# Attention probabilities transposed by VectorE in 32x32 squares instead of by TensorE and a ScalarE copy

## What is computed

```python
x = x + 0.5 * swiglu(rmsnorm(x, norm_ffn1[l]), w1_gate[l], w1_up[l], w1_down[l])
h = rmsnorm(x, norm_mix[l])
proj = h @ w_in[l]
q, k, v, u = jnp.split(proj, [ATTN_WIDTH, 2 * ATTN_WIDTH, 3 * ATTN_WIDTH], axis=-1)
...
    s_own = jnp.einsum('bhqd,bhpd->bhqp', qc, k_own).astype(jnp.float32) * scale
    s_own = jnp.where(k_pos[None, :] <= q_pos[:, None], s_own, NEG_INF)
    p = jax.nn.softmax(jnp.concatenate([s_sel, s_own], axis=-1), axis=-1)
...
            + jnp.einsum('bhqp,bhpd->bhqd', p_own, v_own))
...
pooled = multiscale_pool(u, pool_w[l], pool_scale[l])
x = x + jnp.concatenate([attn, pooled], axis=-1) @ w_out[l]
x = x + 0.5 * swiglu(rmsnorm(x, norm_ffn2[l]), w2_gate[l], w2_up[l], w2_down[l])
```

## The kernel before

| piece | engine | work | line |
|---|---|---|---|
| 36 | PE | scores q·k, two matmuls | L508 |
| 40 | DVE | scale and mask, row maxima | L1208, L1213 |
| 41 | ACT | exponential with row sums | L829 |
| 41 | DVE | reciprocal, rows scaled: `probs` | L1220, L1225 |
| 39 | PE | three 128x128 transposes of `probs` into PSUM | L520 |
| 43 | ACT | copy to SBUF: `probsT` | L837 |
| 43 | PE | values: v·`probsT`, two matmuls | L530, L532 |
| 47 | ACT | rounding into `h` | L842 |
| 48 | DVE | rest into `h`, signals `attn_ready` | L1231 |

## Time and profile before

### The profile page before, as it was taken

One profiled execution on the slowest core, in us unless ns is written; L12 is line 12 of the kernel. 1 busy time (PEld: TensorE's weight loads), 2 busy tenths in 40 slices (PEclk: granted clock), 3 DMA queues, 4 the chain that ended last, 5 costly groups with the idle time before them and its releaser, 6 DMA issues.

```text
span 1743.6 us, 20419 instructions
## 1 busy us (share of the span) xinstructions
PE 1733.9 (99%) x7878; PEld 1442.8 (83%) x7878; DVE 1118.7 (64%) x1378; ACT 782.5 (45%) x892; POOL 20.4 (1%) x24
## 2 busy tenths in 40 slices
PE   9999999999999999999999999999999999999998
PEld 7888888888888888888888888888888888888886
DVE  5666666666665566577676866666666666654554
ACT  6444444444444444454544555444444444443443
POOL 0000000000000000000040000000000000000000
PEclk9999999999999999999999999999999999999999
DMA  8555555555555555666544555555555555565552
GB/s 292 194 193 192 193 193 193 192 193 193 194 196 193 193 194 194 213 195 193 169 161 154 193 192 193 194 192 193 193 192 192 192 192 192 200 210 193 193 193 97
DMA packets 174257, 334.51 MB, mean 192 GB/s; under 512 B 5672, under 2 KB 17408, under 8 KB 174080
## 3 DMA queue, kind: packets, MB, share of 16 engines
q1 hardware_dynamic: 172608, 332.51, 56.2%
q10 hardware_dynamic: 1600, 1.32, 0.2%
HBM read 331.71 MB, written 2.10 MB: 191 GB/s over the span
## 4 chain that ended last, share of the span: by engine, by line
PE 99%; DMA 0%; DVE 0%; ACT 0%; SPq 0%; issue 0%; ACTq 0%
PE banks L389 30%; PE banks L391 30%; PE banks L390 30%; PE banks L375 5%; PE banks L378 3%; PE banks L545 0%; DMA raw<-in_w_gate 0%; PE banks L508 0%; PE banks L530 0%; PE banks L520 0%; PE banks L427 0%; PE banks L532 0%; PE banks L442 0%; DVE w_lo L881 0%; ACT w_hi L651 0%
## 5 line engine op out<-in xcount | busy, mean ns | idle before, releaser
L881 DVE TENSOR_TENSOR w_lo<-raw,w_hi 128x1024 fp32r<-128x1024 f32 x623 | 762.7, 1226 | 590.3 <-ACT w_hi L651 589.0
L651 ACT ACTIVATE w_hi<-raw 128x1024 fp32r<-128x1024 f32 x623 | 659.6, 1060 | 924.7 <-PE banks L391 848.2
L389 PE MATMUL banks<-w_hi,act 128*128 128x512 f32 x1468 | 572.7, 390 | 0.3 <-DVE act L895 0.3
L391 PE MATMUL banks<-w_lo,act 128*128 128x512 f32 x1468 | 571.4, 389 | 0.0
L390 PE MATMUL banks<-w_hi,act 128*128 128x512 f32 x1468 | 571.3, 389 | 0.0
L389 PE MATMUL banks<-w_hi,h 128*128 128x512 f32 x832 | 324.3, 390 | 0.0
L390 PE MATMUL banks<-w_hi,h 128*128 128x512 f32 x832 | 323.8, 389 | 0.0
L391 PE MATMUL banks<-w_lo,h 128*128 128x512 f32 x832 | 323.7, 389 | 0.0
L389 PEld LDWEIGHTS banks<-w_hi,act 128*128 128x128 f32 x1468 | 275.6, 188 | 57.5 <-DVE act L895 0.5
L391 PEld LDWEIGHTS banks<-w_lo,act 128*128 128x128 f32 x1468 | 275.5, 188 | 57.3
L390 PEld LDWEIGHTS banks<-w_hi,act 128*128 128x128 f32 x1468 | 275.6, 188 | 56.7
(11 more groups left out here) (125 smaller groups left out, 372.2 us busy)
## 6 DMA issues: line engine op xcount, KB each, us to landing
raw<-in_w_up SPq DMA_DIRECT2D x88, 1024.0 KB, 5.0
raw<-in_w_down SPq DMA_DIRECT2D x88, 1024.0 KB, 5.0
raw<-in_w_gate SPq DMA_DIRECT2D x84, 1024.0 KB, 5.0
raw<-in_w_in SPq DMA_DIRECT2D x32, 1024.0 KB, 5.4
raw<-in_w_out SPq DMA_DIRECT2D x16, 1024.0 KB, 5.0
raw<-in_w_gate SPq DMA_DIRECT2D x7, 512.0 KB, 8.7
xr<-in_x SPq DMA_DIRECT2D x8, 256.0 KB, 8.1
out<-out_rows SPq DMA_DIRECT2D x8, 256.0 KB, 2.5
```

What stands on the lines that cost most here:

```text
L389: pe.matmul(dst, operand[:, k, hi], w_hi[:, s, w], start=k == first, stop=False)
L391: mm = pe.matmul(dst, operand[:, k, hi], w_lo[:, s, w], start=False, stop=k == last)
L651: act_e.activation(w_hi[:, s, :], raw[:, (p // 2) % RAW_SLOTS, off:off + PIECE], ACT.Copy).then_inc(hi_ready, 1)
L881: dve.tensor_tensor(w_lo[:, s, :], raw[:, (p // 2) % RAW_SLOTS, off:off + PIECE], w_hi[:, s, :].bitcast(F32), ALU.subtract).then_inc(lo_re ...
```

## The change

The three transposes on TensorE (L520) and ScalarE's copy (L837) go away, with the semaphore between them. In their place VectorE writes `probsT` straight from `probs` in SBUF, 16 instructions for each head: each takes 32 partitions and 32 columns of each of the three blocks (32 x 96 values). They are given out in two parts of eight, at VectorE's pieces 42+3·hd and 43+3·hd. VectorE no longer waits for TensorE's transposes before it overwrites `probs`, and the values of head 0 take over the wait for `quad_read`, which the first transpose had.

```diff
-SCORES_AT, TURN_AT, VALUES_AT = 36, 39, 43
+SCORES_AT, TURN_AT, VALUES_AT = 36, 42, 43
...
-            def head_turn(hd):
-
-                pe.wait_ge(probs_ready, hd + 1)
-                if hd == 0:
-                    pe.wait_ge(quad_read, 4)
-                else:
-                    pe.wait_ge(probsT_ready, hd)
-                for j in range(3):
-                    mm = pe.transpose(banks[:, 2, j * P:(j + 1) * P],
-                                      probs[:, hd % 2, j * P:(j + 1) * P], ident[:, :])
-                mm.then_inc(probs_turned, 1)
-
             def head_values(hd):
                 pe.wait_ge(probsT_ready, hd + 1)
                 pe.wait_ge(v_ready, 2 if hd < 4 else 4)
+                if hd == 0:
+                    pe.wait_ge(quad_read, 4)
                 if hd >= 1:
                     pe.wait_ge(attn_ready, hd)
...
-                    hd = (p - TURN_AT - 4) // HEAD_STEP
-                    if (p - TURN_AT - 4) % HEAD_STEP == 0 and 0 <= hd < HEADS:
-                        act_e.wait_ge(probs_turned, hd + 1)
-                        if hd >= 2:
-                            act_e.wait_ge(values_ready, hd - 1)
-                        act_e.activation(probsT[:, hd % 2, :], banks[:, 2, 0:3 * P],
-                                         ACT.Copy).then_inc(probsT_ready, 1)
...
+            def turn_probs(hd, part):
+
+                dve.wait_ge(probs_ready, hd + 1)
+                if hd >= 2:
+                    dve.wait_ge(values_ready, hd - 1)
+                for m in range(8 * part, 8 * part + 8):
+                    i, j = m // SB, m % SB
+                    rows, cols = slice(j * SQ, (j + 1) * SQ), slice(i * SQ, (i + 1) * SQ)
+                    ins = dve.transpose(
+                        probsT[cols, hd % 2, :].rearrange("p (b q) -> p b q", b=3)[:, :, rows],
+                        probs[rows, hd % 2, :].rearrange("p (b q) -> p b q", b=3)[:, :, cols])
+                if part == 1:
+                    ins.then_inc(probsT_ready, 1)
...
-                        if hd >= 2:
-                            dve.wait_ge(probs_turned, hd - 1)
                         dve.wait_ge(scores_ready, hd + 1)
...
+                    for part in range(2):
+                        hd = (p - TURN_AT - part) // HEAD_STEP
+                        if (p - TURN_AT - part) % HEAD_STEP == 0 and 0 <= hd < HEADS:
+                            turn_probs(hd, part)
```

More of the change, by code:

```diff
@@ L242, in layer_kernel @@
         probs_ready = sem("probs_ready")
-        probs_turned = sem("probs_turned")
         probsT_ready = sem("probsT_ready")
@@ L609, in middle @@
                         head_scores((p - SCORES_AT) // HEAD_STEP)
-                    if (p - TURN_AT) % HEAD_STEP == 0 and 0 <= (p - TURN_AT) // HEAD_STEP < HEADS:
-                        head_turn((p - TURN_AT) // HEAD_STEP)
                     if (p - VALUES_AT) % HEAD_STEP == 0 and 0 <= (p - VALUES_AT) // HEAD_STEP < HEADS:
```

## The result

The changed kernel takes 1754.53 us (median of 4 runs, 1753.56 to 1755.27) against 1745.71 us before: 1.0049 times the time, 95% interval 1.0037 to 1.0061, so 8.8 us slower. The forecast was 1756.2 us, in a range of 1751 to 1762.

What follows compares the result with a forecast made beforehand. TensorE, busy 99% of the span, was taken to bound the kernel until VectorE's new work, 37.9 us, exceeded its 27.4 us reserve; the 10.5 us excess on the median gave 1756.2 us, range 1751 to 1762, TensorE's saved 2.6 us vanishing in waits.

Steps and rivals of the forecast that it cites:

- VectorE's reserve of 27.4 us: VectorE's idle time before its splits, from piece 42's split to head 7's write; new work would use it up.
- the fall of the clock: Rival: TensorE's clock drops to half speed behind its new waits, at most 16 us on top, 1772 us; 5%.
- the signs that were to show me wrong: Transpose below 0.2 us, idle time left before splits, clock below 1.00 in the stretch, or TensorE waiting for `w_lo`.
- The price of a transpose: Each 32x96 transpose on VectorE: 270 ns, 0.28 us with the gap, for 128 of them.
- The second item: On VectorE, overlap lost between split and transpose: 0.12 us for each of 16 parts, 1.9 us more work.
- Waits left at the end: VectorE's waits left behind the last transposes, before head 7's write: 0 to 1.5 us, taken as 0.
- TensorE's waits: About 13.4 us (10.5 + 2.6 + 0.3), before the values, released by the write into `h`.
- the wait at piece 67: TensorE's existing wait for `h` at the output projection, 0.3 us, added into its expected idle time.
- the reserve is enough: Rival: cheap transposes fill only VectorE's idle time, so 2.6 us are won, 1743.1 us; 6%.
- A price independent of the width: Rival: each transpose on VectorE costs 0.4475 us whatever its width, +31.8 us, 1777.5 us; 4%.
- GpSimd does not slow the transposes: Rival claimed the opposite: transposes double during GpSimd's pooling windows, 9 us more, 1765.2 us; 5%.

Runs made afterwards that it cites:

- half: Changed kernel with 8 of the 16 transposes of each head left out, 64 in all, so probabilities are incomplete: 1743.93 us, ratio 0.9989.
- added_only: Kernel before with everything left in it and the 128 transposes added on VectorE, written to memory nothing reads: 1753.30 us, ratio 1.0044.
- removal_only: Kernel before without TensorE's transposes and ScalarE's copy, nothing put in their place, so attention's result differs: 1743.18 us, ratio 0.9986.
- narrow: Changed kernel with all 16 transposes per head 32x32 instead of 32x96, so probabilities are incomplete: 1748.39 us, ratio 1.0015.
- fill_three: Changed kernel with unread matmuls of ones on TensorE ahead of the values of heads 4, 5 and 6: 1753.46 us, ratio 1.0044.
- hybrid_five: Changed kernel with heads 0, 1, 2, 4, 6 on VectorE, `h` write first; others on TensorE with ScalarE's copy, one piece later than before: 1744.07 us, ratio 0.9990.
- fill: Changed kernel with unread matmuls of ones on TensorE ahead of the values of heads 4 and 6: 1754.26 us, ratio 1.0046.
- write_first: Changed kernel with the write into `h` put ahead of the eight transposes of the same step: 1753.48 us, ratio 1.0045.
- causal: Changed kernel with 6 of each head's 16 transposes shortened from 32x96 to 32x32, the result the same: 1751.88 us, ratio 1.0035.

## Why the prediction was right

The direction and the mechanism held: VectorE's reserve of 27.4 us, counted in one stretch from a point that VectorE reaches at the same time in both kernels to one where it sets the time, was what the new work had to fit into. half, added_only and removal_only show that threshold: 0 transposes −2.5 us, 64 of them −1.7 us, 128 of them +8.8 us, and still +7.6 us with TensorE's work put back or with the clock kept up. Without the fall of the clock the sum is VectorE's new work less its reserve, and no more.

That the forecast of 10.5 us lies within 2 us of the measured 8.8 is in part luck. The mechanism gives 7.6 us; the rest came from the clock, a rival that I had given 5% and left out of the sum. The range would have held 7.6 us as well (1753.3 us). Two of the signs that were to show me wrong appeared: a clock below 1.00 in the stretch, and 1.5 us of idle time before the splits at its end.

*The price of a transpose.* Predicted 270 ns and 0.28 us with the gap; measured 269 ns and 0.28 us. It came from one longer row of the same instruction and a slope from others. The 32x32 form of narrow, 202 ns, gives the slope of the transposes themselves: (269 − 202)/64 = 1.05 ns per element, with 169 ns fixed. The Trainium skill's table ("VectorE: DVE Perf Modes", section on the TRN2 errata) would have had 160 ns, an estimate by which the change is a gain; the fixed term of about 150 cycles, which the page has as measured, gives an estimate of 256 ns and comes near. By it the prediction's sum gives 128 · 0.2675 + 1.9 − 27.4 = +8.7 us, where the text has +8.6.

*The second item was wrong.* I added 1.9 us for overlap lost between split and transposes. The part behind a split costs no overlap (the split at 862.31 is followed after 1.13 us), and the other part loses a few hundredths. More than that, I forgot that filling idle time gives overlap back: where the write into `h` stood before an idle time it took 0.42 us, now the split starts 0.34 us behind it (865.69 to 866.03). VectorE's time outside its waits for ScalarE rose from 88.34 − 27.4 = 60.9 us to 97.58 − 1.7 = 95.9 us, so the new work came to 34.9 us and not 37.9. The transposes alone are 34.4 us busy and have 1.7 us of gaps before them, 36.1 us in all, where I had 36.0. Everything else that VectorE does in the stretch came to 1.6 us less busy time (93.14 − 34.4 = 58.7 us where it was 60.33) and 0.4 us more gaps. The overlaps given back and one slow pair of L1217 less beside GpSimd make the 1.6. So the second item was −1.2 us and not +1.9.

*Waits left at the end.* I had allowed for 0 to 1.5 us and taken 0. In the rows 1.7 us are left. 0.2 us of it stand before the first split and were no reserve before the change either. The other 1.5 us belong to the clock: with the clock at 1.00 (fill_three) none are left behind the first split, so 0 was right for the mechanism that I had summed. The sum of the rows is 34.9 − 27.4 + 1.7 = 9.2 us, where I had 37.9 − 27.4 = 10.5. The new work was 3.0 us less than forecast; the clock took back 1.5 us of that difference, and the 0.2 us that were no reserve the rest.

*TensorE's waits.* Predicted 13.4 us before the values of heads 1 to 6; 7.3 us stand there in the timeline. Place and releaser were right, the size was not. For one thing the loss was smaller. For another, the 0.3 us of the wait at piece 67 should not have been added, since that wait is still there, as long as before (the same 0.41 and 0.34 us between starts, now at 939.83 and 940.24). That leaves 9.24 + 2.64 = 11.9 us to account for. Of these, 7.3 us are the waits, 1.4 us what stopping and going on costs beside them, and 3.2 us the two falls of the clock. By head the waits were 0.2 to 0.8 us for heads 1 to 3 where I had 1 to 1.5 us, and 2.9, 0.85 and 2.2 us for heads 4 to 6.

*The rivals.* That the reserve is enough holds only for a cheaper or smaller job (half). A price independent of the width is ruled out by narrow. GpSimd does not slow the transposes (275 ns the longest of 128), though it slows splits. The fall of the clock, to which I gave 5%, did happen, behind two of six waits, and 1.5 us of it showed in the profiled execution; I had priced it at up to 16 us by letting every wait have one. That the clock also comes back to 1.00 once TensorE has worked on, the prediction's rows could not show; the windows from 904 and from 928 us do.

## What to carry to other kernels

Before moving work to an idle engine, count its idle time in the stretch where the work will stand, from a point that the new work cannot move to one where that engine already sets the time, and compare sums there: well below the reserve the move was all but free (64 transposes), well above it the excess showed whole (7.6 us at full clock). Close to it (narrow) both engines had waits, and the time was 2.5 us longer although new work and reserve were nearly equal. One instruction into many short ones is dear when each has a fixed part (169 of 269 ns here), so it pays to move only as many pieces as the reserve holds, as in hybrid_five, and leave the rest where they were. And a wait of TensorE of 2 us or more may cost again in the clock behind it.

## What was new about the hardware

The granted clock fell to 0.50 for about 3 us behind waits of 2.90 and 2.21 us in the changed kernel, and fell likewise behind one of 2.48 us in fill and those of 2.70 and 2.23 us in write_first. It is not the length of the wait alone. In causal TensorE waits 2.83 and 2.09 us before the values of two heads:

```profile
898.12 0.67 PE L519 MATMUL banks<-probsT,v 128*128 128x256 f32 x2 [2.83 <-DVE h L1230]
...
910.12 1.03 PE L519 MATMUL banks<-probsT,v 128*128 128x256 f32 x2 [2.09 <-DVE h L1230]
```

and the windows behind them, the granted clock again in the column before the DMA share, are:

```profile
899.00:902.00 3.00, 3.00 (x19) 2.63 (x18) 2.85 (x11) 1.38 (x6) 0.00 (x0) 1.00 0.25 96
910.50:913.50 3.00, 3.00 (x10) 2.50 (x9) 2.87 (x9) 1.21 (x5) 2.92 (x2) 0.50 0.32 91
```

It stays at 1.00 behind the longer wait and falls behind the shorter one. What else decides, no run here shows. No fall was seen behind waits of up to 1.89 us in added_only and narrow. The Trainium skill, "TensorE: Matmul & The Clock Gate", Part 1, says that an idle TensorE is throttled to half rate; the falls agree with it, and what was new to me is that so short a pause between stretches of full work can be enough.

GpSimd and VectorE slow each other, depending on which of their instructions meet. Splits of 1.23 us took up to 2.06 us in narrow, and the pair of row scalings 1.3 to 1.5 us and not 0.55, while transposes kept their 0.27 us. GpSimd's copy of 128x4 took 1.10 us in the kernel before and 0.19 us at the same place in the changed one (890.40).
